# The pooling mix of a hybrid decoder layer: from fp32 products to split fp32r ones, with the attention loop's fills in a new order

## The reference

```python
def pool_mixer(u, pool_w, pool_scale):        # 4 groups of 128 channels, windows 2, 4, 8, 16
    cs = jnp.cumsum(u, axis=1)
    for g, w in enumerate(POOL_WINDOWS):      # trailing mean less the token
        outs.append((cs_g - shifted) / cnt - u[..., sl])
    d = jnp.stack(outs, axis=2)
    y = jnp.einsum('bsgc,gcd->bsgd', d, pool_w).reshape(B, S, POOL_WIDTH)
    return y * pool_scale
...
y_pool = pool_mixer(u_pool, pool_w[l], pool_scale[l]) @ w_pool_out[l]
y_fox = forgetting_attention(q, k, v, f_logit + b_forget[l]) @ w_fox_out[l]
gates = jax.nn.sigmoid(g_logit + b_gate[l])
x = x + (g_pool * y_pool + g_fox * y_fox) @ w_out[l]
```

## Time and profile before

| | |
|---|---|
| median of three | 1502.97 us |
| the profiled execution itself | 1501.31 us |
| its span (first to last instruction) | 1499.5 us |
| TensorE busy | 1434.1 us (96%) |
| weight loads (beside TensorE) | 1182.8 us (79%) |
| VectorE busy | 997.9 us (67%) |
| ACT busy | 626.8 us (42%) |
| POOL busy | 500.0 us (33%) |
| chain that ended last | TensorE 84%, VectorE 6%, ACT 5%, POOL 3% |

### The profile page before, as it was taken

The page is one execution under the profiler, slowest core; times in us unless marked ns, Lnnn a source line. Parts: engine busy times, 40 slices in busy tenths (PEclk is TensorE's granted clock), DMA queues, the critical chain, the costliest instruction groups (busy, mean ns, idle before and its releaser), DMA issues.

```text
span 1499.5 us, 19159 instructions
## 1 busy us (share of the span) xinstructions
PE 1434.1 (96%) x7124; PEld 1182.8 (79%) x7124; DVE 997.9 (67%) x1384; ACT 626.8 (42%) x1173; POOL 500.0 (33%) x386
## 2 busy tenths in 40 slices
PE   6999999999899999999989799999999999999996
PEld 4768888888687878887878588888888888877785
DVE  6858495646776745326654776776776777678956
ACT  6544343536876542125442442222222222434444
POOL 5633233330110001014011744554454443359103
PEclk9999999999999999999999899999999999999998
DMA  9254354445322145114102022332333335862433
GB/s 218 63 97 110 64 119 107 71 106 176 99 99 85 50 153 198 57 56 127 40 32 109 32 96 81 106 106 105 106 106 105 106 105 215 315 227 78 109 96 132
DMA packets 104684, 167.25 MB, mean 112 GB/s; under 512 B 7049, under 2 KB 62857, under 8 KB 103185
## 3 DMA queue, kind: packets, MB, share of 16 engines
q1 hardware_dynamic: 97872, 145.54, 32.9%
q0 software_dynamic: 3312, 11.58, 2.2%
q10 hardware_dynamic: 3408, 8.91, 1.5%
HBM read 123.78 MB, written 42.24 MB: 111 GB/s over the span
## 4 chain that ended last, share of the span: by engine, by line
PE 84%; DVE 6%; ACT 5%; POOL 3%; issue 1%; DMA 1%; POOLq 0%; SPq 0%; DVEq 0%; ACTq 0%
PE ps L1942 25%; PE ps L1944 25%; PE ps L1943 25%; PE ps L2128 2%; PE ps L2137 2%; DVE t_lo L1355 1%; ACT prob L1130 1%; DVE s_lo L1355 1%; ACT prob_t L1121 1%; PE ps L1989 1%; PE ps L2171 1%; PE ps L2172 1%; POOL w_lo L771 1%; POOL rstd L763 1%; PE ps L2011 0%
## 5 line engine op out<-in xcount | busy, mean ns | idle before, releaser
L1942 PE MATMUL ps<-t_lo,s_hi 128*128 128x512 f32 x308 | 120.6, 392 | 4.2 <-DVE t_lo L1355 3.9
L1944 PE MATMUL ps<-t_hi,s_lo 128*128 128x512 f32 x308 | 119.9, 389 | 0.0
L1943 PE MATMUL ps<-t_hi,s_hi 128*128 128x512 f32 x308 | 119.9, 389 | 0.0
L1942 PE MATMUL ps<-h_lo_T,w_hi 128*128 128x512 f32 x256 | 101.2, 395 | 4.8 <-issue 3.8
L1288 ACT ACTIVATE s_hi<-w_raw 128x512 fp32r<-128x512 f32 x77 | 48.7, 632 | 130.0 <-PE ps L1944 110.4
L1944 PE MATMUL ps<-h_hi_T,w_lo 128*128 128x512 f32 x256 | 100.4, 392 | 0.0
L1943 PE MATMUL ps<-h_hi_T,w_hi 128*128 128x512 f32 x256 | 100.4, 392 | 0.0
L1355 DVE TENSOR_TENSOR s_lo<-w_raw,s_hi 128x512 fp32r<-128x512 f32 x77 | 66.0, 857 | 51.3 <-ACT s_hi L1288 51.3
L1304 ACT ACTIVATE p_sb<-ps 128x512 f32<-128x512 f32 x22 | 13.0, 598 | 188.1 <-PE ps L1944 188.1
L771 POOL TENSOR_TENSOR w_lo<-w_raw,w_hi 128x1024 fp32r<-128x1024 f32 x11 | 26.7, 2426 | 190.2 <-ACT w_hi L961 190.2
L1942 PE MATMUL ps<-hf_lo_T,w_hi 128*128 128x512 f32 x212 | 82.5, 389 | 0.0
(11 more groups left out here) (361 smaller groups left out, 4211.1 us busy)
## 6 DMA issues: line engine op xcount, KB each, us to landing
w_raw<-hs_dram SPq DMA_DIRECT2D x77, 256.0 KB, 2.7
raw_p<-in_w_ffn_in SPq DMA_DIRECT2D x22, 512.0 KB, 4.6
w_raw<-in_w_ffn_in SPq DMA_DIRECT2D x22, 512.0 KB, 4.2
hs_dram<-h_sum SPq DMA_DIRECT2D x11, 1024.0 KB, 9.1
hs_dram<-hq SPq DMA_DIRECT2D x11, 768.0 KB, 7.0
wq_B<-in_w_ffn_out SPq DMA_DIRECT2D x8, 1024.0 KB, 8.1
raw_f<-in_w_in SPq DMA_DIRECT2D x14, 512.0 KB, 6.9
gate_dram<-c_st SPq DMA_DIRECT2D x28, 256.0 KB, 2.1
```

Source lines behind the costliest of these rows:

```text
L1942: nc.tensor.matmul(dst, w_h, x_l, start=start, stop=False, skip_group_check=onto)
L1943: nc.tensor.matmul(dst, w_h, x_h, start=False, stop=False, skip_group_check=onto)
L1944: return nc.tensor.matmul(dst, w_l, x_h, start=False, stop=stop, skip_group_check=onto)
```

## The change

The mixing product's weights `pool_w` become a weight chunk, `C_PW` = 0, of half the width (512 columns); all other chunks move up by one. `d` is loaded into the place of `d_lo`; ACT writes `d_hi` group by group in units 4 to 7, VectorE the low part over it in units 5 to 8, and each of the eight mixing products is an `mm3`. Beside that:

- ACT's chunk splits stand at the start of the unit in `SPLIT_AT`, not at its end; a split of `C_PW` in unit 4 is new.
- The two halves of `q2` are zeroed by VectorE at the end of unit 1, not by POOL.
- POOL's queue has the split of `C_PW` between `negc` 2 and 3, and otherwise the order of before.
- VectorE's `qk_lo_of` stands at the end of the unit for all `i`.
- From part 24 on the fills follow another table. Pieces per unit from 12 to 31, before: 2 2 4 4, 2 2 4 4 4 2 2 4, 4 4 4 4 4 2 2 4; now 2 4 4 3, 3 4 2 4 3 3 4 2, 4 3 3 4 2 4 3 3.

```diff
-C_PO = 0
+C_PW = 0
+C_PO = C_PW + 1
...
-SPLIT_AT = {8: 0, 10: 1, 12: 2, 18: 3, 23: 4, 28: 5, 32: 6}
+SPLIT_AT = {4: 0, 8: 1, 10: 2, 12: 3, 18: 4, 23: 5, 28: 6, 32: 7}
...
-    FILL.append(FILL[-1] + (FIRST_FILL + NEXT_FILL)[part])
+    FILL.append(FILL[-1] + (FIRST_FILL[part] if part < 29 else (2, 2, 1, 1, 2)[(part - 24) % 5]))
...
                     for g in range(NG):
-                        sp.dma_start(d_in_sb[:, g, :], d_dram[g]).then_inc(d_in[g // 2], 16)
-                    sp.dma_start(pw_sb[:], pool_w.rearrange("g c d -> c g d")).then_inc(d_in[0], 16)
+                        sp.dma_start(d_lo[:, g, :].bitcast(FP32), d_dram[g]).then_inc(d_in[g // 2], 16)
...
-            for a in range(2):
-                other = slice((1 - a) * DH, (2 - a) * DH)
-                pool.wait_ge(q2_zeroed, 2 + a)
-                nc.gpsimd.memset(q2[1][a][other, :].bitcast(FP32), 0.0).then_inc(q2_zeroed, 1)
             pool.wait_ge(op_lo, N_FRONT)
             load_negc(2)
+            split_lo(0)
             load_negc(3)
             load_negc(4)
-            pool.wait_ge(q2_zeroed, 4)
-            for n in range(3):
+            for n in range(1, 4):
                 split_lo(n)
             load_negc(5)
             load_negc(6)
-            split_lo(3)
             split_lo(4)
+            split_lo(5)
             load_negc(7)
...
             for u in range(PAIRS * T + 1):
                 p, i = divmod(u, T)
-                if u == PAIRS * T:
+                if u in SPLIT_AT:
                     split_hi(SPLIT_AT[u])
...
                 copy_groups(groups[2:])
+                if 4 <= u < 8:
+                    act.wait_ge(d_in[(u - 4) // 2], 32)
+                    nc.scalar.activation(d_hi[:, u - 4, :], d_lo[:, u - 4, :].bitcast(FP32), ACT.Copy).then_inc(d_hi_ready, 1)
...
-                if u in SPLIT_AT and u < PAIRS * T:
-                    split_hi(SPLIT_AT[u])
...
-                if i >= 4 and u < 3 * T and i - 1 in SPLIT_HI:
-                    e, a0, a1 = SPLIT_HI[i - 1]
-                    qk_lo_of(p + 1, e, (qk_st if p else qk_first)[:, e % 2, :], a0, a1)
                 for a in range(2 if u < PAIRS * T else 0):
                     dve.wait_ge(exp_ready, 2 * u + a + 1)
...
+                if u == 1:
+                    dve.wait_ge(f_ev, FEV["C11", LAST_PAIR])
+                    zero_q2(1)
+                if 5 <= u < 9:
+                    g = u - 5
+                    dve.wait_ge(d_hi_ready, g + 1)
+                    minus_hi(d_lo[:, g, :], d_lo[:, g, :].bitcast(FP32), d_hi[:, g, :], d_lo_ready)
...
-                if i < 4 and u < 3 * T and i - 1 in SPLIT_HI:
+                if u < 3 * T and i - 1 in SPLIT_HI:
                     e, a0, a1 = SPLIT_HI[i - 1]
                     qk_lo_of(p + 1, e, (qk_st if p else qk_first)[:, e % 2, :], a0, a1)
...
-                    pe.wait_ge(d_in[0], 48)
-                    pe.wait_ge(d_in[1], 32)
+                    pe.wait_ge(lo_ready, C_PW + 1)
+                    pe.wait_ge(d_lo_ready, g + 1)
...
-                    nc.tensor.matmul(ps[:, MIX_BANK[m % 3], :], pw_sb[:, g, :], d_in_sb[:, g, half_of(h)],
-                                     start=True, stop=True).then_inc(mix_done, 1)
+                    last = mm3(ps[:, MIX_BANK[m % 3], :], w_hi[C_PW % SLOTS][:, tile_of(g)], w_lo[C_PW % SLOTS][:, tile_of(g)],
+                               d_hi[:, g, half_of(h)], d_lo[:, g, half_of(h)], True, True)
+                    last.then_inc(mix_done if m < 7 else w_used, 1)
```

More of the change, by code:

```diff
@@ L284, in build @@
         d_lo = place("d_lo", 16, [P, NG, S], F32R)
-        d_in_sb = place("d_in_sb", 16, [P, NG, S])
-        pw_sb = place("pw_sb", 14, [P, NG, P])
         qk_first = place("qk_first", 148, [P, 2, HALF])
@@ L388, in build @@
         vt_done, v_copied = sem("vt_done"), sem("v_copied")
-        d_in, mix_done, mix_hi, mix_lo = [sem(f"d_in{i}") for i in range(2)], sem("mix_done"), sem("mix_hi"), sem("mix_lo")
+        d_in, d_hi_ready, d_lo_ready, mix_done, mix_hi, mix_lo = ([sem(f"d_in{i}") for i in range(2)], sem("d_hi_ready"), sem("d_lo_ready"),
+                                                                  sem("mix_done"), sem("mix_hi"), sem("mix_lo"))
         g_in = [sem(f"g_in{i}") for i in range(2)]
@@ L437, in chunk_view @@
         def chunk_view(k):
+            if k == C_PW:
+                return pool_w.rearrange("g c d -> c g d")
             if k < C_FO:
@@ L454, in chunk_view, with width @@
             raise ValueError(k)
+        def width(k):
+            return NG * P if k == C_PW else 1024
         block = ctx.enter_context(nc.Block())
@@ L544, in load_raw @@
                     sp.wait_ge(s_sum, 4 * NF)
-                sp.dma_start(w_raw[n % RAWS][:], chunk_view(n)).then_inc(raw_loaded[n % RAWS], 16)
+                t = w_raw[n % RAWS][:, 0:width(n)]
+                if n == C_PW:
+                    t = t.rearrange("p (k n) -> p k n", n=P)
+                sp.dma_start(t, chunk_view(n)).then_inc(raw_loaded[n % RAWS], 16)
             def front_view(g, half, c0, c1):
@@ L770, in split_lo @@
                     pool.wait_ge(lo_ready, n)
-                nc.gpsimd.tensor_tensor(w_lo[n % SLOTS][:], w_raw[n % RAWS][:], w_hi[n % SLOTS][:].bitcast(FP32), ALU.subtract).then_inc(lo_ready, 1)
+                w = width(n)
+                nc.gpsimd.tensor_tensor(w_lo[n % SLOTS][:, 0:w], w_raw[n % RAWS][:, 0:w], w_hi[n % SLOTS][:, 0:w].bitcast(FP32),
+                                        ALU.subtract).then_inc(lo_ready, 1)
             def front_sum(g, i):
@@ L830, in _ @@
             load_negc(1)
-            pool.wait_ge(f_ev, FEV["C11", LAST_PAIR])
-            pool.wait_ge(s_sum, 4 * NF)
-            for a in range(2):
-                other = slice((1 - a) * DH, (2 - a) * DH)
-                pool.wait_ge(q2_zeroed, 2 + a)
-                nc.gpsimd.memset(q2[1][a][other, :].bitcast(FP32), 0.0).then_inc(q2_zeroed, 1)
             pool.wait_ge(op_lo, N_FRONT)
             load_negc(2)
+            split_lo(0)
             load_negc(3)
             load_negc(4)
-            pool.wait_ge(q2_zeroed, 4)
-            for n in range(3):
+            for n in range(1, 4):
                 split_lo(n)
@@ L960, in split_hi @@
                     act.wait_ge(prod_done, (N_STAGE + 2, N_FRONT, N_STAGE)[n])
-                nc.scalar.activation(w_hi[n % SLOTS][:], w_raw[n % RAWS][:], ACT.Copy).then_inc(hi_ready, 1)
+                w = width(n)
+                nc.scalar.activation(w_hi[n % SLOTS][:, 0:w], w_raw[n % RAWS][:, 0:w], ACT.Copy).then_inc(hi_ready, 1)
             def square(n, src, junk):
@@ L1133, in _ @@
                 copy_groups(groups[2:])
+                if 4 <= u < 8:
+                    act.wait_ge(d_in[(u - 4) // 2], 32)
+                    nc.scalar.activation(d_hi[:, u - 4, :], d_lo[:, u - 4, :].bitcast(FP32), ACT.Copy).then_inc(d_hi_ready, 1)
                 for m in MIXED_IN.get(u, ()):
                     g, h = divmod(m, 2)
-                    act.wait_ge(mix_done, m + 1)
+                    if m < 7:
+                        act.wait_ge(mix_done, m + 1)
+                    else:
+                        act.wait_ge(w_used, C_PW + 1)
                     nc.scalar.activation(d_hi[:, g, half_of(h)], ps[:, MIX_BANK[m % 3], :], ACT.Copy,
```

10 lines of the change are left out of this document (5 added, 5 removed).

## The result

The changed kernel took 1515.32 us (median of 4 executions, 1514.13 to 1516.68), the kernel before 1503.26 us beside it (4 executions, 1501.31 to 1505.09). The ratio is 1.0083, with a 95% interval of 1.0068 to 1.0097: some 12 us slower. The forecast was 1506.3 us in a range of 1500.0 to 1510.5, and "no change" as the likeliest case.

A forecast was written before the change was run, and what follows sets the result against it. TensorE, busy 1434.1 of 1499.5 us, was taken as the bound. The terms summed to +3.4 us on the profiled 1501.31, giving 1504.7; the median's offset of 1.66 made it 1506.3 us, range 1500.0 to 1510.5.

The forecast's parts named there:

- q2 zeroed by VectorE: End of unit 1: two memsets on VectorE delay unit 2's bias step, about +0.7 us.
- fp32r mixing product and its splits on ACT and VectorE: Units 4 to 11: cheaper products save 0.35 us on TensorE, ACT's added splits in units 4 to 8 cost 1.9.
- k's low half behind the normalisation: Unit 7 into 8: k's low half is ready late, so unit 8's scores wait 0.76 us, counted +0.8.
- early splits, bias row of head 7: Units 23 and 28: earlier splits end unit 24's bias-row waits, -2.0 us, and a 0.42 us wait at 515.80.
- fill table: Units 15, 23, 31: fewer pieces under ACT's long exponentials lengthen the waits for `prob_t`, +2.76 us.
- the port collision: Unit 8: POOL's split of C_PO gets ahead of k's low half, VectorE waits 2.36 us; +5.7, 1508.7 us; chance 0.20.
- The new work on ACT and VectorE: Units 4 to 8: ACT's five more instructions exceed its idle time in units 4 and 5, +1.9 us.
- The third rival: Units 4 and 5: TensorE's lead hides the new ACT and VectorE work; 1503.0 us; chance 0.12.
- The second rival: Unit 24: head 7's bias row `negc` is late all the same, the 2.0 us stay; +5.4, 1508.4 us; chance 0.08.
- The subtraction stretched by POOL in unit 28: VectorE's subtraction took 2.56, not 1.22 us, during POOL's split; moving the split removes TensorE's wait, -0.42 us.
- The fourth rival: Attention loop: fills pay more than the idle rows show, mixing gives its full -1.4; -4.9, 1498.1 us; chance 0.12.
- The offset of the median: Whole kernel: the median lies 1.66 us above the profiled execution, and the same was added to the forecast.

The follow-up runs named there:

- e3: Changed kernel with the old fill table and the low halves of q and k back before the normalisation for i >= 4: 1504.12 us, ratio 1.0001.
- e7: Changed kernel with old fill table, low halves of q and k before the normalisation for i >= 4, q2 zeroed on POOL: 1502.76 us, ratio 0.9988.
- e6: Kernel before with all of ACT's chunk splits at the start of the unit: 1501.56 us, ratio 0.9982.
- e1: Changed kernel with the fill table of before, all else changed: 1506.66 us, ratio 1.0016.
- e4: Kernel before with the new fill table and nothing else: 1523.74 us, ratio 1.0123.
- e2: Changed kernel with the low halves of q and k back before the normalisation for i >= 4: 1513.33 us, ratio 1.006.
- e8: Kernel before with the bias row of head 7 loaded ahead of the split of chunk 4: 1500.74 us, ratio 0.9981.
- e9: Kernel before with only the chunk splits of units 23 and 28 moved to the unit's start: 1500.95 us, ratio 0.9976.

## Why the prediction was wrong, step by step

The sum against what the kernels differ by at unit 31:

| step | predicted | measured | from |
|---|---|---|---|
| q2 zeroed by VectorE | +0.7 | +1.4 | e3 less e7 |
| fp32r mixing product and its splits on ACT and VectorE | -0.35 + 1.9 | +2.4: -0.3 + 1.1, and 1.6 of clock | e7 less e6 |
| k's low half behind the normalisation | +0.8 | +2.65 | e1 less e3 |
| early splits, bias row of head 7 | -2.0 - 0.42 | -2.65 | e6 less before |
| fill table | +2.76 | +9.0 | after less e1 |
| sum | +3.4 | +12.8 | |

- **The step that failed is the fill table**, "What counts is the pieces of the units with `i` = 7, since these stand under ACT's two long exponentials". It priced a piece as cover that is missing elsewhere, and this came out: 0.81, 1.70 and 1.00 us. It did not ask what a piece waits for itself. The answer was in the kernel's text, one wait on `za_done` ahead of each result's first piece, and in the earlier trace rows, which show the old table paying nothing for it. Measured: +9.0 us where the sum has +2.76, 5.55 of them waits for `za`, and e1 and e4 show from both sides that the table is the cause.
- **The late low half of k** was forecast to cost 0.76 us of waiting, with the port collision as a rival at 0.20. The rival is what happened: 2.55 us, and 0.57 more in the wait before it (2.53, in e2 and e3 1.96). These 3.1 us are what e1 and e3 differ by at unit 9 (7.01 - 3.89); 0.6 of them is made good by unit 16. Its condition was that ACT's split is over before VectorE takes up the second k instruction, and it was over 0.7 us before. The text itself said that this is within 0.5 us either way; 0.20 was too little for that. The argument against it, that the instruction that holds has the right of way, is true and doesn't help between two instructions.
- **The new work on ACT and VectorE** was counted in the right place and too high: 1.9 us, where TensorE is 1.13 late at the end of unit 7 in e7. The third rival, that it is hidden, is out by the same number. The products' own gain came as forecast: e7 is 2.74 us behind e6 at unit 8, 2.43 at unit 16, -0.3 against -0.35.
- **The clock** was in no step, and it is why that row of the table is 0.8 us over its forecast and not under it: 1.6 us of TensorE's work behind the wait of 1.96 us at the end of unit 7. The changed kernel and e1 had their fall a little later, behind the wait for k, so e1 and e3 both have one by unit 9 and it is not in the 2.65. Why it fell behind 1.96 us in e2, e3 and e7 and not in the kernel before or e6 no run shows; each has one trace.
- **q2**: the two memsets started 1.18 us apart though each is listed at 0.91, so they took 2.0 us from 355.19 to the bias step at 357.20. I had 1.8, and TensorE waited 1.14 us for the bias step.
- **The bias row of head 7** was right: predicted -2.0, measured -2.2 from unit 24 to 25 in the changed kernel, e6, e8 and e9. The second rival (it is late all the same) is out.
- **The subtraction stretched by POOL in unit 28** was put at -0.42, by the one idle row of TensorE. e9 gains 3.47 - 2.46 = 1.0 us from unit 28 to 31, and e8, which does not move that split, nothing.
- The fourth rival (the table pays) is refuted by e4. The offset of the median, +1.66, stands: outside the loop the profiled spans of the eleven kernels are 1.2 to 6.1 us longer than that of before, 2.3 in the middle, with the same instructions. In the changed kernel some of this is the clock again, 0.98 from 687 to 760 us where before's trace has 1.00.

What stays open: all of the table's 9.0 us arise between the first bias steps of units 12 and 31. TensorE's time there, in the changed kernel and in e1 (columns as in the earlier trace rows):

```profile
415.51:534.68 119.17, 110.74 (x827) 91.82 (x827) 76.08 (x184) 77.14 (x178) 11.68 (x7) 1.00 0.23 76
```

```profile
415.57:525.75 110.18, 109.10 (x832) 91.83 (x833) 77.05 (x185) 76.83 (x178) 11.72 (x7) 1.00 0.25 82
```

It idles 8.43 us and 1.08, a difference of 7.35, of which the rows explain 5.55 for `za` and 0.35 + 1.23 for `prob_t`, together 7.1. It is also busy 1.64 us longer, and one piece, 0.69, is the reason for part of that: by unit 31 the new table has done 85 of the 88 and the old one 84. The last 1 us isn't found. The table was not tried with a second bank for the results.

## What to carry to other kernels

Before a filler instruction is moved on a busy in-order engine, list what it waits for, and put the release of its buffer on the same time line: a result that begins right behind the last one in the same bank costs a full hand-over, and if the release stands behind another engine's work, that too. One cause of delay can cost more once the order behind it has no slack: the same late DMA cost 2.2 us with the old table and 7.0 with the new one, so fix lateness before tightening the order. A rival whose condition lies within half a microsecond of the sum deserves about even odds.
